# Three moves in a two-block network kernel: the embedding's operands, the positions network and extra products around the norm spreads

## The reference

```
h = h + g1 * hyena_mixer(a, ...)          # first block, second layer
hdn = sin(freq * (z @ w1 + b1)); hdn = sin(freq * (hdn @ w2 + b2)); hdn = sin(freq * (hdn @ w3 + b3))
h_filt = (hdn @ filt_out) * window        # filters of the long convolutions, z: 33 position features
h = h + g2 * swiglu(modulate(h, ...), w1, w3, w2)
...
h = h + 0.5 * swiglu_2(rms_norm(h, ffb_norm[i]), w_gate_up, w_down)      # second block, network "b"
gate = sigmoid(rms_norm(h, ple_norm[i]) @ ple_w_gate[i])                # 1024 x 1024
h = h + gate * (p[i] @ ple_w_proj[i])                                   # the embedding: 256 x 1024
return rms_norm(h, final_norm)
```

## Time and profile before

| | us |
|---|---|
| median of 3 runs (4157.44 to 4158.93) | 4158.46 |
| the profiled execution, its own time | 4156.04 |
| its span in the trace | 4154.2 |
| TensorE busy in it | 3963.3 (95%) |
| VectorE, ScalarE, GpSimd busy | 2038.6, 1314.0, 457.4 |

### The profile page before, as it was taken

The page is one execution under the profiler, slowest core; times in us unless marked ns, Lnnn a source line. Parts: engine busy times, 40 slices in busy tenths (PEclk is TensorE's granted clock), DMA queues, the critical chain, the costliest instruction groups (busy, mean ns, idle before and its releaser), DMA issues.

```text
span 4154.2 us, 47658 instructions
## 1 busy us (share of the span) xinstructions
PE 3963.3 (95%) x19618; PEld 3262.3 (79%) x19618; DVE 2038.6 (49%) x3065; ACT 1314.0 (32%) x1964; POOL 457.4 (11%) x509
## 2 busy tenths in 40 slices
PE   8988889999989999999999989999999999999997
PEld 5678889788867887888888766888778878778886
DVE  6545565646356765433443444433543343553445
ACT  3225344322232223222322345322332232342223
POOL 0015543100001111000200034000100000010001
PEclk9899999999999999999999999999999999999999
DMA  6220002445231112332322311232232223012322
GB/s 208 77 71 1 1 1 92 129 150 188 83 108 50 45 42 92 99 104 90 103 92 90 103 59 41 90 104 77 96 108 91 90 83 103 21 52 91 105 79 75
DMA packets 344098, 351.26 MB, mean 85 GB/s; under 512 B 9547, under 2 KB 340107, under 8 KB 343628
## 3 DMA queue, kind: packets, MB, share of 16 engines
q1 hardware_dynamic: 343884, 348.22, 26.2%
HBM read 345.83 MB, written 2.10 MB: 84 GB/s over the span
## 4 chain that ended last, share of the span: by engine, by line
PE 89%; DVE 5%; ACT 3%; issue 2%; DMA 1%; POOL 0%; POOLq 0%; SPq 0%; DVEq 0%; ACTq 0%
PE ps L371 23%; PE ps L372 23%; PE ps L373 23%; PE ps L1495 4%; PE ps L2417 3%; PE ps L2374 1%; PE ps L378 1%; ACT whi L347 1%; PE ps L3292 1%; PE ps L458 1%; PE ps L460 1%; PE ps L459 1%; DVE wlo L353 1%; PE ps L3279 1%; PE ps L764 1%
## 5 line engine op out<-in xcount | busy, mean ns | idle before, releaser
L353 DVE TENSOR_TENSOR wlo<-raw,whi 128x2048 fp32r<-128x2048 f32 (+6 forms) x315 | 627.7, 1993 | 988.7 <-ACT whi L347 988.7
L371 PE MATMUL ps<-Xh,whi 128*128 128x512 f32 x2640 | 1042.4, 395 | 23.8 <-DVE wlo L353 10.0
L372 PE MATMUL ps<-Xl,whi 128*128 128x512 f32 x2640 | 1034.6, 392 | 0.0
L373 PE MATMUL ps<-Xh,wlo 128*128 128x512 f32 x2640 | 1034.2, 392 | 0.0
L347 ACT ACTIVATE whi<-raw 128x2048 fp32r<-128x2048 f32 (+6 forms) x315 | 521.8, 1656 | 1127.2 <-PE ps L373 1114.2
L371 PEld LDWEIGHTS ps<-Xh,whi 128*128 128x128 f32 x2640 | 499.5, 189 | 137.0 <-issue 31.2
L372 PEld LDWEIGHTS ps<-Xl,whi 128*128 128x128 f32 x2640 | 499.5, 189 | 105.9 <-issue 2.0
L373 PEld LDWEIGHTS ps<-Xh,wlo 128*128 128x128 f32 x2640 | 499.0, 189 | 106.4 <-issue 0.5
L371 PE MATMUL ps<-HDh,whi 128*128 128x512 f32 x1056 | 411.7, 390 | 0.0
L373 PE MATMUL ps<-HDh,wlo 128*128 128x512 f32 x1056 | 410.9, 389 | 0.0
L372 PE MATMUL ps<-HDl,whi 128*128 128x512 f32 x1056 | 410.8, 389 | 0.0
(11 more groups left out here) (556 smaller groups left out, 5592.4 us busy)
## 6 DMA issues: line engine op xcount, KB each, us to landing
raw<-in_ffn_w SPq DMA_DIRECT2D x44, 1024.0 KB, 5.3
raw<-in_ffa_w_gate_up SPq DMA_DIRECT2D x44, 1024.0 KB, 5.0
raw<-in_ffb_w_gate_up SPq DMA_DIRECT2D x44, 1024.0 KB, 5.0
mslot<-in_mod_w SPq DMA_DIRECT2D x28, 1024.0 KB, 7.9
raw<-in_mod_w SPq DMA_DIRECT2D x20, 1024.0 KB, 6.0
raw<-in_ab_w_in SPq DMA_DIRECT2D x14, 1024.0 KB, 5.2
raw<-in_ffn_w SPq DMA_DIRECT2D x16, 768.0 KB, 4.4
raw<-in_hy_w_in SPq DMA_DIRECT2D x12, 1024.0 KB, 5.1
```

Of the source, the lines that this page charges most:

```text
L353: dve.tensor_tensor(k.part(k.wlo, c), k.raw(c), k.part(k.whi, c).bitcast(F32), ALU.subtract).then_inc(*k.ev.put("dve_wlo", ("lo", n), ("ra ...
L371: pe.matmul(o, wh, xh, start=first, stop=False)
L372: pe.matmul(o, wh, xl, start=False, stop=False)
L373: return pe.matmul(o, wl, xh, start=False, stop=last)
```

## The change

It has five parts.

1. The embedding's projection becomes one chunk of 2 x 1024 columns, placed in the list before the third output pair of part 1 of network `b`. It is not in the ring of split slots: ScalarE and VectorE split it (`ple_up_act`, `ple_up_dve`) into tiles of `X` that the network has finished with. The embedding itself is fetched and split (`ple_in_act`, `ple_in_dve`) at hidden column 7 of network `b`. In the embedding stage only the four gate chunks use the slots.
2. The positions network's three layers run in `f0` after hidden columns 7, 8 and 9, with their constants fetched before. The first filters come between the second and the third projection.
3. For n1, n2, n3, n6 and n10 TensorE does 2 products of 512 columns between the sum and the spread and 8 after the spread (`keep_busy_pe`); nobody reads them.
4. For n13 GpSimd adds only tiles 0 to 5 and TensorE sums tiles 6 and 7 itself; the load of the root's table is put ahead of the last two squares.
5. The final scaling: VectorE copies the spread and does six tiles, ScalarE and GpSimd do tiles 6 and 7, and eight DMAs of 256 KB store the tiles.

```diff
                 W.add((st, "g", c), wg, lead, 0, 8, c * 256, 256)
                 W.add((st, "u", c), wu, lead, 0, 8, uoff + c * 256, 256)
             for cc in range(4):
+                if (st[0], part, cc) == ("b", 1, 2):
+                    W.add(("pu" + st[1], 0), "ple_w_proj_2", lead, 0, 2, 0, D, False)
                 for q in range(2):
                     W.add((st, "d", part, cc, q), wd, lead, (c0 * 2 + q * nch) * 128, nch, cc * 256, 256)
...
-            W.add(("pu%d" % li, cc), "ple_w_proj_2", (li,), 0, 2, cc * 256, 256)
     return W
...
+NEXT_CHUNK = {"n1": ("f0", "g", 0), "n2": ("hy", 0, 0), "n3": ("f1", "g", 0), "n6": ("cq", 0), "n10": ("fq", 0)}
+def keep_busy_pe(k, pe, tag, n, last):
+    c = k.W[NEXT_CHUNK[tag]]
+    if last:
+        ps = k.bk.of(("busy", tag))
+    else:
+        ps = room(k, pe, ("busy", tag))
...
+    w = k.whi[c.n % NH]
+    for i in range(n):
+        ins = pe.matmul(ps[:, :], w[:, 0:128], w[:, 0:512], start=True, stop=True)
+    if last:
+        ins.then_inc(*k.ev.put("pe_busy", ("out", "busy", tag)))
 def early_pe(k, pe, tag):
-    ps = k.psum[NB]
-    for last, src, there in ((0, k.sq[2], ("sqsum", tag, 6)), (1, k.sq[1], ("sq", tag, 7))):
+    ps, n = k.psum[NB], pool_squares(tag)
+    parts = [(k.sq[2], ("sqsum", tag, n - 1))] + [(k.sq[m % 2], ("sq", tag, m)) for m in range(n, 8)]
...
         pe.wait_ge(*k.ev.at(there))
         for t in range(4):
             o = slice(t * 128, t * 128 + 128)
-            ins = pe.matmul(ps[:, t:t + 1], src[:, o], k.onesD[:, 0:1], start=(last, t) == (0, 0), stop=(last, t) == (1, 3))
+            ins = pe.matmul(ps[:, t:t + 1], src[:, o], k.onesD[:, 0:1], start=(i, t) == (0, 0),
+                            stop=(i, t) == (len(parts) - 1, 3))
     ins.then_inc(*k.ev.put("pe_sum", ("summed", tag, 7)))
+    if tag in NEXT_CHUNK:
+        keep_busy_pe(k, pe, tag, 2, False)
     ps = room(k, pe, ("rs", tag))
     pe.wait_ge(*k.ev.at(("rcol", tag)))
     for t in range(4):
         ins = pe.matmul(ps[:, t * 128:t * 128 + 128], k.rcol[:, t:t + 1].to_broadcast([128, 128]), k.ident[:, :], start=True,
                         stop=True)
     ins.then_inc(*k.ev.put("pe_sum", ("rstd", tag)))
+    if tag in NEXT_CHUNK:
+        keep_busy_pe(k, pe, tag, 8, True)
...
+            if st == "f0" and 7 <= c < 10:
+                place_pe(k, pe, c - 7)
             if step is not None:
...
+            if st[0] == "b" and c == 7:
+                ple_in_act(k, act, int(st[1]))
         for cc in range(4):
+            if st[0] == "b" and (part, cc) == (1, 1):
+                ple_up_act(k, act, int(st[1]))
...
+    k.hw1 = k.sb("hw1", [64, 3, 64], R0 + 113 * K)
+    k.zps = k.sb("zps", [128, L], R0 + 114 * K)
+    k.ptmp = k.sb("ptmp", [64, L], R0 + 116 * K)
     k.zt = k.sb("zt", [128, 4, 256], R0 + 108 * K)
     k.win = k.sb("win", [128, 4, 256], R0 + 112 * K)
...
         yield "project", 0, part
-        yield "place", part, None
         if part == 0:
             yield "fetch", 0, None
-    yield "filters", 0, None
+        if part == 1:
+            yield "filters", 0, None
     yield "kspec", 0, None
...
+def place_sp(k, sp):
+    ev = k.ev
+    sp.wait_ge(*ev.at(("h", "n1", 7)))
     sp.dma_start(k.zps[0:33, :], k.I["zpos"]).then_inc(*ev.put("d_zpos", ("in", "zpos"), n=16))
     sp.dma_start(k.hw1[:, :, :], k.I["hyw"]).then_inc(*ev.put("d_hyw", ("in", "hyw"), n=16))
...
+    ev = k.ev
+    if s == 0:
+        for x in ("zpos", "hyw"):
+            pe.wait_ge(*ev.at(("in", x)))
+    else:
+        pe.wait_ge(*ev.at(f"hd{s}"))
+    ps = room(k, pe, ("hp", s))
+    rows = 64 if s else 33
+    pe.matmul(ps[0:64, :], k.hw1[0:rows, s, :], (k.hdT if s else k.zps)[0:rows, :], start=True, stop=True).then_inc(
+        *ev.put("pe_hy", ("mm", "hp", s)))
+def place_act(k, act, s):
+    act.wait_ge(*k.ev.at(("hp", s)))
+    act.activation(k.hdT[:, :], k.hdT[:, :], ACT.Sin).then_inc(*k.ev.put("act_hy", f"hd{s + 1}"))
 def spectrum_pe(k, pe, group, ri, a, src):
...
 def ple_mem(k):
     k.pT = k.sb("pT", [128, 2, L], R0 + 114 * K)
-    k.PX = k.two("PX", 36 * K, 2)
+    k.PX = (k.sb("PXh", [128, 2, L], R0 + 52 * K, F32R), k.sb("PXl", [128, 2, L], R0 + 76 * K, F32R))
...
+def ple_in_act(k, act, li):
+    ev = k.ev
+    act.wait_ge(*ev.at(("in", "p", li)))
+    act.wait_ge(*ev.at(("mm", "b%d" % li, "d", 0, 7)))
+    act.activation(k.PX[0][:, :, :], k.pT[:, :, :], ACT.Copy).then_inc(*ev.put("act_ple", ("px hi", li)))
...
+def ple_up_act(k, act, li):
+    ev, c = k.ev, k.W[("pu%d" % li, 0)]
+    act.wait_ge(*ev.at(("raw", c.j)))
+    act.wait_ge(*ev.at(("mm", "b%d" % li, "u", 10, 1)))
+    act.activation(k.PU[0].rearrange("p c k n -> p k c n"), up_raw(k, c), ACT.Copy).then_inc(
+        *ev.put("act_ple", ("pu hi", li)))
...
+    dve.wait_ge(*ev.at(("pu hi", li)))
+    dve.tensor_tensor(k.PU[1].rearrange("p c k n -> p k c n"), up_raw(k, c),
+                      k.PU[0].bitcast(F32).rearrange("p c k n -> p k c n"), ALU.subtract).then_inc(
+        *ev.put("dve_ple", ("pu", li), ("raw free", c.j)))
...
-                ins.then_inc(*ev.put("pe_ple", ("mm", st, cc * 2 + s), *([("used", c.n)] if s else [])))
-            if (cc, st) == (0, g):
-                gained_sum_pe(k, pe, norm)
+        c = k.W[(g, cc)]
+        hi, lo = k.hi(c), k.lo(c)
+        for s in range(2):
+            ps = room(k, pe, (g, cc * 2 + s))
+            o = slice(s * 128, s * 128 + 128)
+            if s == 0:
+                pe.wait_ge(*ev.at(("lo", c.n)))
+            for kk in range(8):
+                if cc == 0 and s == 0:
+                    pe.wait_ge(*ev.at(("x", norm, kk)))
+                ins = mm3(pe, ps[:, :], hi[:, kk, o], lo[:, kk, o], X[0][:, kk, :], X[1][:, kk, :], kk == 0, kk == 7)
+            ins.then_inc(*ev.put("pe_ple", ("mm", g, cc * 2 + s), *([("used", c.n)] if s else [])))
+        if cc == 0:
+            gained_sum_pe(k, pe, norm)
+            pe.wait_ge(*ev.at(("px", li)))
+            pe.wait_ge(*ev.at(("pu", li)))
+        for s in range(2):
+            ps = room(k, pe, (u, cc * 2 + s))
+            o = slice(s * 128, s * 128 + 128)
+            for kk in range(2):
+                ins = mm3(pe, ps[:, :], k.PU[0][:, cc, kk, o], k.PU[1][:, cc, kk, o], k.PX[0][:, kk, :], k.PX[1][:, kk, :],
+                          kk == 0, kk == 1)
+            ins.then_inc(*ev.put("pe_ple", ("mm", u, cc * 2 + s)))
     if tag in EARLY:
         early_pe(k, pe, tag)
 def ple_act(k, act, li, norm, tag):
-    ev, g, u = k.ev, "pg%d" % li, "pu%d" % li
-    act.wait_ge(*ev.at(("in", "p", li)))
-    act.activation(k.PX[0][:, :, :], k.pT[:, :, :], ACT.Copy).then_inc(*ev.put("act_ple", ("px hi", li)))
+    ev, g = k.ev, "pg%d" % li
...
+        if cc == 3 and tag in EARLY:
+            root_table(k, act)
         for s in range(2):
             m = cc * 2 + s
...
                 early_sq_act(k, act, tag, m)
+    next_hi(k, act, (g, 3))
 def ple_dve(k, dve, li, norm, tag):
     ev, g, u = k.ev, "pg%d" % li, "pu%d" % li
-    dve.wait_ge(*ev.at(("px hi", li)))
...
     for cc in range(4):
-        next_lo(k, dve, (g, cc))
+        if cc < 3:
+            next_lo(k, dve, (g, cc))
         if cc == 0:
...
-                next_lo(k, dve, (u, cc))
             buf, h = k.gr[m % 4], k.h[:, m, :]
             dve.wait_ge(*ev.at(("mm", u, m)))
...
...
         load_mod(k, sp, x, MODS_PROJ)
+    place_sp(k, sp)
...
     upto(("mo0", 0), 1)
     even_mla_sp(k, sp)
-    upto(("pg0", 0))
+    upto(("b0", "g", 2))
     ple_sp(k, sp, 0)
     upto(("fq", 0))
     odd_sp(k, sp)
     upto(("fv", 0), 3)
     odd_mask_sp(k, sp)
-    upto(("pg1", 0))
+    upto(("b1", "g", 2))
     ple_sp(k, sp, 1)
-    upto(("pu1", 3), 1)
+    upto(("pg1", 3), 1)
     assert n[0] == len(W.list)
-    sp.wait_ge(*k.ev.at(("h", "out", 7)))
-    sp.dma_start(k.out.rearrange("(k p) t -> p k t", p=128), k.h[:, :, :]).then_inc(*k.ev.put("d_out", "stored", n=16))
-    sp.wait_ge(*k.ev.at("stored"))
+    out = k.out.rearrange("(k p) t -> p k t", p=128)
+    for i in (0, 1, 2, 3, 6, 4, 5, 7):
+        sp.wait_ge(*k.ev.at(("h", "out", i)))
+        sp.dma_start(out[:, i, :], k.h[:, i, :]).then_inc(*k.ev.put("d_out", ("stored", i), n=16))
+    sp.wait_ge(*k.ev.at(("stored", 7)))
...
 def scaled_h_dve(k, dve, norm, gain, tag):
...
+    dve.tensor_copy(k.rstd[:, :], rs_of(k, norm)).then_inc(*k.ev.put("dve_h", ("rs copy", norm)))
+    for i in range(6):
         dve.scalar_tensor_tensor(k.h[:, i, :], k.h[:, i, :], k.col(gain, i), rs_of(k, norm), ALU.mult, ALU.mult).then_inc(
-            *k.ev.put("dve_h", ("h", tag, i), *rs_done(k, norm, i == 7)))
+            *k.ev.put("dve_h", ("h", tag, i)))
+def scaled_h_act(k, act, norm, gain):
+    for i in (6, 7):
+        act.activation(k.h[:, i, :], k.h[:, i, :], ACT.Copy, scale=k.col(gain, i)).then_inc(
+            *k.ev.put("act_out", ("gained", norm, i)))
+def scaled_h_pool(k, pool, norm, tag):
+    pool.wait_ge(*k.ev.at(("rs copy", norm)))
+    for i in (6, 7):
```

(2 more changed lines are left out.)

78 lines of the change are left out of this document (36 added, 42 removed).

## The result

The changed kernel took 4102.0 us (median of 4 executions, 4100.8 to 4121.8), the kernel before beside it 4158.7 (4157.4 to 4161.8): ratio 0.987, 95% interval 0.9854 to 0.9885. The forecast was 4104, range 4095 to 4117. Measured again in a later session, the changed kernel took 4114.1 (5 executions, 4100.8 to 4123.9) beside 4163.0, ratio 0.9883 (0.9865 to 0.9900). So the gain is 49 to 57 us by the medians; between the fastest executions of each it is 56.6 us in the first session (4157.4 and 4100.8) and 54.2 in the second (4155.0 and 4100.8).

A forecast was written before the change was run, and what follows sets the result against it. TensorE bounds the kernel almost throughout; gains come from its waits and half clock. Terms 19.5 + 17.6 + 10.0 + 6.0 = 53.1 us off 4156.04 give 4102.9, stated as 4104; own range 4099 to 4109, with rivals 4095 to 4117.

The forecast's parts named there:

- The embedding stages: 19.5 expected: Both embedding stages: TensorE waits of 10.0 and 6.1 us go, with the half clock behind them; bounds 13 to 21.
- the price of a restart: Embedding stages: each TensorE restart after a hole also loses 0.16 us, counted only in the upper bound of 21.
- the two terms of 1.7: Embedding stages: half clock behind the waits, worth 1.7 us in each of the two stages.
- The Hyena stage: 17.6 expected: Third layer to first spectrum: 30.0 us less filters 4.2, full-clock spectrum 7.1 and moved layer 1.1; bounds 14 to 18.
- the one for what becomes late behind the change: Hyena and f0: VectorE's chain delays a split by some 1.2 us without harm; window products might wait 3 us.
- The products: 10.0 expected: Five norms: extra products let the clock rise about when real work starts, 2.0 us a norm; bounds -5.5 to 14.
- The real start isn't later by 0 to 0.9 us: Norms: eight products, 1.8 to 3.4 us against a hole of 2.54, delay real work 0 to 0.9 us.
- the pair, from which I counted the unbroken work: Norms: TensorE works without a hole from the two products ahead of the spread; clock rises 3.6 to 5.5 us later.
- the clock never falls: Rival at the norms: the pair bridges the pause enough, 4 to 6 us more won, 4099; chance 0.12.
- The end: 6.0 expected: Last norm and output: sums 1.4 us, scaling and DMAs 4.3, spread 0.3 at a guess; bounds 3 to 8.
- the late splits: Rival: splits come late at two embedding stage ends and in f0, 10 us in all, 4114; chance 0.10.
- the clock at the norms: Rival: the extra products don't raise the clock earlier, part 3 worth 0 to -5.5 us, 4116; chance 0.13.

The follow-up runs named there:

- place_alone: Kernel before with only part 2 (positions network's layers in f0, filters ahead of the third projection): 4151.6 us beside 4159.0, ratio 0.9976.
- after_again: The changed kernel unaltered, measured again in a later session: 4114.1 us (4100.8 to 4123.9) beside 4163.0, ratio 0.9883.
- eight_only: Changed kernel with the eight products behind each spread but without the two ahead of it: 4110.5 us beside 4163.0, ratio 0.9885.
- bank_turn: Changed kernel with two PSUM banks instead of one for the products at n1, n2 and n3: 4108.9 us beside 4160.6, ratio 0.9875.
- attention_fill: Changed kernel plus seven unused 512-column products behind the last attention's first pair of products: 4110.5 us beside 4160.4, ratio 0.9873.
- end_alone: Kernel before with only parts 4 and 5 (squares, table load, final scaling and DMAs): 4155.8 us beside 4159.0, ratio 0.9989.
- bank_shift: Kernel before plus one 512-column product, taking a PSUM bank, behind each of the five spreads: 4157.2 us beside 4160.6, ratio 0.9994.

## Why the prediction was right, point by point

**The embedding stages: 19.5 expected, 21.6 measured** (13.1 and 8.5, in nine traces). Right, and too low by 2.1: the waits and the half clock come to 11.7 and 7.8 us as the prediction had them, and the rest fits the price of a restart. I had set it at 0.16 us in the bounds; over the eight waits it is 2.1 / 8 = 0.26 us each. The first product after a hole also takes 0.31 us to the next one instead of 0.227 (1196.89 at n2 of after, with the next at 1197.20), which makes it 0.24. It stood in the bound and not in the sum. The half clock in it, 3.4 us by the two terms of 1.7, was in this trace of before and isn't in every one, as said above.

**The Hyena stage: 17.6 expected, 16.2 measured** (19.8 less the 3.6 that f0 grew by). Right for the wait, the full clock of the spectrum and f0, where nothing became late, though its three layers cost 3.6 us and not 3 x 1.07 = 3.2. The term that failed is the one for what becomes late behind the change: 1.2 us at `zt`. The spectrum now starts while VectorE still has a weight split and the work of the third projection to do; GpSimd's `Kf` beside it take up to 1.86 us instead of 0.72, and ScalarE's two buffers wait for them. In the trace before, TensorE's wait of 10.33 us had let VectorE finish all of that first. This is read from the rows of both traces and from place_alone, which has the same 1.86 us and the same wait of 2.05; no run takes the VectorE work away. I had looked at the filters' products with the window and not at what follows the spectrum. Where the clock falls right behind (3.4 us near 1250, in six of the nine traces with the moved layers) another 1.6 us go.

**The products: 10.0 expected, 10.4 measured in the profile, 8.1 in after_again.** The mechanism is the one I gave: the clock falls and rises about when real work starts, with 3.4 us of half clock or none in the profile instead of 6.8 to 10.2. Two details of the working were wrong in opposite directions. The real start isn't later by 0 to 0.9 us, as VectorE's first tile sets it. And the pair, from which I counted the unbroken work, adds nothing to the eight: eight_only has the same half clock at all five norms as after_again. In these two, bank_turn and attention_fill it lasts 6.8 us at n2 and n6, which makes most of the difference between 10.4 and 8.1 (3.1 us less won at these two, 0.7 more at n3). What the eight replace is the hole behind the spread. In one of five norms (n2) the clock didn't fall in the profile, in after_again it fell there: my rival "the clock never falls" is true by chance, place by place, and not for all norms at once.

**The end: 6.0 expected, 4.7 measured, 6.4 in end_alone and bank_turn.** The scaling with its DMAs gave 4.1 of the 4.3 expected. By the Trainium skill (SBUF — State Buffer, Who interferes with whom) GpSimd's tiles wouldn't be held up by the scaling; the trace agrees: 2.49 us for two, 1.25 each, and VectorE 4.03 for six, the same 0.67 as the earlier trace rows have. The sums ahead of the spread gave 0.6 instead of 1.4 in the profile, as the clock fell ahead of the last of them. The table load is where it should be, 4082.36; the operation ahead of it ends at 4082.34 and the next one starts at 4083.65, so the whole switch takes 1.31 us and no drain is seen.

**What no term had: 2.3 us at the output projection of the last attention**, 470 us ahead of the end and with no line of the diff in it. The five banks taken at the norms shift the turn of all later ones. I had read the order of the instructions without the numbers of the banks. Also outside the terms: half clock of 3.4 us that stood in the Hyena stage's last part (1593 us in before) isn't in after's trace (-1.5), and 1.0 us was lost ahead of n1, where nothing was changed.

**The sum.** 21.6 + 16.2 + 10.4 + 4.7 = 52.9, against 53.1 predicted; with 2.3 and 1.5 from outside and 1.5 lost in small things it is the 55.2 by which the spans differ. The errors of the four terms, +2.1, -1.4, +0.4 and -1.3, cancelled each other: that the sum is right to 0.2 us is luck, the terms are right to 0.4 to 2.1. So is it that the forecast met the median to 2 us. In the session of the 4102.0 three of four executions lay at 4101 to 4102; the second session gives 12 us more. The range, 4095 to 4117, was built without that: it covered the late splits and the clock at the norms, and holds the second session's median by 3 us only. What was missing was a term for an execution's own spread, for which the trace of before gave a sign: in it half clock comes in 28 separate stretches.

## What to carry to other kernels

Take the value of a part from the same instruction in two traces, stage by stage, and not from the time of the kernel: four parts won 36.9 us alone and 49 to 57 together, while the three with a trace had their own stage's gain in it within 1.7 us of what the whole shows there. When TensorE has a pause that can't be removed, fill it up to the real start with products (512 columns here, no other width was tried): that shortened half clock at five of five norms, while two products ahead of the spread alone did so at one. When an engine's wait goes, look at what the other engines had done in it: the 10.33 us were also the time in which VectorE got out of GpSimd's way. And when a change takes a buffer from a rotation, compare the numbers of the buffers in everything that comes later: five extra banks were worth 2.3 us in a stage that nobody had touched.

## What the runs showed of the hardware

GpSimd and VectorE slow each other in some pairs of instructions. GpSimd's additions of 128x256 took 0.90 to 1.86 us beside VectorE's work on operands in SBUF, and 0.72 without it; VectorE's took 0.95 and 1.09 us there instead of 0.49 and 0.75. Beside the final scaling, which reads one operand from SBUF and one from PSUM, neither was longer: GpSimd's two tiles of 128x512 took 1.26 us each, an addition of that size with VectorE idle takes 1.27 to 1.29, and VectorE stayed at 0.67.

The granted clock isn't a property of the program. The changed kernel, in traces of two executions, stood at 0.97 over the 116 us of the last attention's stage and at 0.85 in the other:

```profile
3503.60:3619.60 116.00, 111.16 (x776) 77.13 (x774) 69.67 (x101) 45.46 (x88) 0.00 (x0) 0.97 0.03 10
```

```profile
3513.80:3643.00 129.20, 124.36 (x774) 87.63 (x773) 70.10 (x101) 45.21 (x88) 0.00 (x0) 0.85 0.03 9
```

TensorE is busy in almost all of both, and its idle time is the same, 4.84 us; the second took 13 us more. Of that stage's 776 products 512 use 64 of 128 rows; they take 53 of its 116 us in before. The columns are 128 to 512. In thirteen traces it had 6.8 us of half clock in seven, and 13.7 to 37.6 in six: three with the wait of 1.8 us near its start (34 to 38 us), two with 1.2 and one with 0.7 (14 to 17). The Trainium skill (TensorE: Matmul & The Clock Gate, What's actually happening) says that the window over which the chip judges activity doesn't begin with the kernel, so that the moment of a change differs between runs; the traces agree as far as they go: 6.8 us of half clock from 3529.6 in the first of the two, 13.7 from 3516.3 and 23.9 from 3547.0 in the second. Which executions fall in this stage stays open: the profiled after and bank_shift had the wait of 1.8 us too and held, so the wait alone isn't enough, and attention_fill held without it.
